# Delta operands stored by pairs of heads, last batches solved in a row, RWKV preparation with fewer products

## The chip, the cores and the metric

One Trainium2 chip, one core. The metric is the device time of one execution in microseconds: median 4167.8 of three runs. TensorE (PE), VectorE (DVE), ScalarE (ACT), GpSimd (POOL) and SyncE (SP, which here only issues DMAs) run their own instruction streams and meet at semaphores.

## The reference, cut to what matters

Two blocks in a row on x of 512 x 2048. The first (convolution, differential attention) and the second's input products are untouched. The change lies in the second block's mixers, each with 512 latent and 256 context tokens, in both directions, in chunks of 64:

```python
def gated_delta_chunked(q, k, v, beta, g, s0):        # 8 heads of 128
    decay = exp(where(tril, g_i - g_j, -inf))
    lmat = where(strict, (k * beta) @ k.T * decay, 0)
    tmat = inverse(eye + lmat)                        # a 64x64 system per head and chunk
    u, wk = tmat @ (v * beta), tmat @ (k * beta * exp(g))
    attn = where(tril, q @ k.T * decay, 0)
    def step(state, inp):                             # 12 chunks in order
        v_new = u_i - wk_i @ state
        o_i = q_i @ state + attn_i @ v_new
        state = state * exp(gl_i) + k_i.T @ v_new

def rwkv7_scan(r, w, k, v, kk, b_vec, s0):            # 16 heads of 64
    def step(state, inp):
        sa = -state @ kk_t
        state = state * w_t + sa x b_t + v_t x k_t
        return state, state @ r_t
# w_log = -softplus(-(w0 + tanh(wd) @ w_up)) - 0.5 ; decay = exp(-exp(w_log))
# so log(decay) = -exp(-0.5) * sigmoid(w0 + tanh(wd) @ w_up)
# context tokens only feed the state: in the last layer their outputs are not needed
```

The kernel brings the RWKV recurrence to chunks too: per chunk two 64x64 matrices from b and two from k (one of each against kk, one against r), and one system to invert.

## The kernel before

It runs in stages with a barrier between them: first block, second block's input products (`second`), `delta_prep`, `rwkv_prep`, `scans`, `closing`. P is 128 partitions, C = 64 tokens, NCH = 12 chunks (8 latent and 4 context), GH = 8 Delta heads, RP = 8 pairs of RWKV heads. A `Link` makes each DVE or POOL instruction wait for the one before it.

**delta_prep** (`DeltaPrep`) goes through the 8 heads; in a round, head i is finished while head i+1 is begun. It writes the head's operands into `ob[:, u]`, 12 x 579 floats a partition: for each direction 129 (`G_CH`: keys, queries, the chunk's decay), then 321 (`G_TOK`: masked matrix, values, tailed keys, beta). SP's `store` sends them to `g_scr` (chunk, head, partition, column) in pieces of 2316 bytes, and the systems' rows from `nb` in pieces of 256 bytes. `finish` waits for all stores before the barrier.

**rwkv_prep** (`RwkvPrep`) goes through 8 units of two heads, again with the next unit's beginning woven in. SP first issues `load_all` (six loads) and then each unit's seven (`load`, four of them gate weights). The DVE order is written out: `unit_keys`, `operands` for both directions, `mask` mb, `add_up` of the next unit, `mask` mk, `add_up`, `mask` mb, `add_bonus`, `mask` mk. The PE products that a `mask` reads wait for the mask before (`m_out`, one buffer `ps_m`). Meanwhile POOL solves systems, 96 at a time on 96 partitions (`solve`: load, wait, `invert`, store, wait): Delta's batch for both directions, then, once units 0 to 3 are stored, RWKV's first batch for both. The stage ends when POOL's last store has landed.

**scans** solves RWKV's second batch on POOL while the scans begin: `solve` d = 0, then d = 1, each waiting for its own load and store, in the one room `r.ops[0:96, 1]`. The loop takes steps n = 0 to NCH + LAG - 1 with LAG = 8: Delta's step n for n < 12 and RWKV's step n - 8 from n = 8. Steps 0 to 3 of each scan are context and produce no output. PE's order in a step: Delta keys, RWKV keys, `middle` and later `offdiagonal` of the next step's inverses, values, then `advance` by halves. RWKV's `middle` of step 0 therefore stands in step n = 7, before Delta's values. From n = 12 one tile of Delta's outputs a step is folded (`fold`, `take`, `add`). SP loads three inverses, then operands of two Delta steps, then in the loop operands of step n + 2 (two buffers, released by `free`); a step's operands are 2 x 528 KB in pieces of 516 bytes (`gchan`) and 2 x 657 KB in pieces of 1284 bytes (`gtok`). At n = LAG - 2 it waits for both solves (`y_out`) and loads RWKV's inverses and its step 1.

Of the kernel before, what the change touches and what calls it, by code (L numbers as in the profile page):

```python
# [21 lines left out]
P = 128  # L22
# [2262 lines left out]
class DeltaPrep:  # L2285
# [5 lines left out]
    def __init__(self, nc, st, k, p2, norms, gates_scr, g_scr, systems):  # L2291
        self.nc, self.k, self.p2, self.norms, self.gates_scr, self.g_scr, self.systems = nc, k, p2, norms, gates_scr, g_scr, systems
# [12 lines left out]
        self.ob = st.sb("ob", [P, 2, NCH, G_COLS])  # L2305
# [5 lines left out]
        self.x_in, self.stored = st.sems("x_in", 3), st.sems("stored", 2)  # L2311
# [135 lines left out]
    def heads(self, dve, i):  # L2447

        u = i % 2
        if i >= 2:  # L2450

            dve.wait_ge(self.stored[u], 48 * (i // 2))
        dve.wait_ge(self.s["eg_out"], 2 * i + 2)
        for d in range(2):
            self.tt(self.ob[:, u, :, G_CH * d:G_CH * d + 2 * C].rearrange("p c (j t) -> p c j t", t=C), self.kq[:, u],
                    self.eg[:, u, d].unsqueeze(2).to_broadcast([P, NCH, 2, C]))

    def weights(self, dve, i):
        u, em = i % 2, self.em[:, i % 2]
        beta = self.gb[:, 1, i, :]  # L2460
        self.link(self.nc.vector.tensor_scalar(self.ob[:, u, :, G_COLS - 1:G_COLS], self.over(beta, 1), 1.0, None, ALU.mult))
# [5 lines left out]
        self.tt(self.ob[:, u, :, 2 * G_CH:2 * G_CH + C], prod[:, :, 1, :], em)  # L2467
# [5 lines left out]
    def tails(self, dve, i):  # L2473
        u = i % 2
        dve.wait_ge(self.s["tok_k"], i + 1)
        self.tt(self.ob[:, u, :, 2 * G_CH + C + GD:2 * G_CH + C + 2 * GD], self.ps_t[:].rearrange("p (c v) -> p c v", v=GD),
# [11 lines left out]
    def exponentials(self, act_e, i):  # L2488
        u = i % 2
        act_e.wait_ge(self.s["em_ok"], i + 1)  # L2490
        if i >= 2:

            act_e.wait_ge(self.stored[u], 48 * (i // 2))
        self.alink(self.nc.scalar.activation(self.em[:, u], self.em[:, u], ACT.Exp))
        self.alink(self.nc.scalar.activation(self.tail[:, u], self.tail[:, u], ACT.Exp))
        self.alink(self.nc.scalar.activation(self.ob[:, u, :, G_CH - 1:2 * G_CH:G_CH], self.total[:, u], ACT.Exp))
        act_e.sem_inc(self.s["em_out"], 1)

    def values_out(self, act_e, i):
        act_e.wait_ge(self.s["tok_v"], i + 1)  # L2500
        self.alink(self.nc.scalar.activation(self.ob[:, i % 2, :, 2 * G_CH + C:2 * G_CH + C + GD],
# [3 lines left out]
    def store(self, sp, i):  # L2505
        u = i % 2
        sp.wait_ge(self.s["k_out"], i + 1)
        sp.dma_start(self.g_scr[:, i:i + 1].rearrange("c h p x -> p (c h) x"), self.ob[:, u]).then_inc(self.stored[u], 16)
        for d in range(2):
            rows = self.systems[d, 0:NCH * GH, :].rearrange("(c h) (s t) -> h s c t", h=GH, t=C)  # L2510
            sp.dma_start(rows[i:i + 1].rearrange("h s c t -> (h s) c t"),
                         self.nb[64 * d:64 * d + 64, u]).then_inc(self.stored[u], 16)

    def finish(self, sp):
        for u in range(2):
            sp.wait_ge(self.stored[u], 48 * GH // 2)


def delta_prep(nc, k, p2, norms, gates_scr, g_scr, systems):


    with Stage(nc, "gprep") as st:
        m = DeltaPrep(nc, st, k, p2, norms, gates_scr, g_scr, systems)
# [122 lines left out]

class RwkvPrep:
# [1197 lines left out]
```

## Time and profile before

| | us |
|---|---|
| median of three runs (lowest to highest) | 4167.8 (4160.57 to 4168.13) |
| the profiled execution, its own time | 4166.44 |
| its span, first to last instruction | 4164.7 |
| PE busy | 3582.6 (86%) |
| DVE busy | 2122.5 (51%) |
| ACT busy | 676.5 (16%) |
| POOL busy | 788.5 (19%) |
| mean granted TensorE clock | 0.917 of full speed |

Busy shares are means over stages with different limits: PE is the bound in the first block, and in the three stages changed here it is not. So they are read by stage.

### The profile page before, as it was taken

The page shows a single profiled execution, that of the slowest core. Times are in us where ns is not written, and L with a number is a line of the kernel's source. Part 1 is how long each engine was busy: PE and PEld are TensorE (multiplying, and loading weights), DVE is VectorE, ACT ScalarE, POOL GpSimd, SP SyncE. Part 2 cuts the span into 40 slices and gives each one's busy share as a digit, 9 for nine tenths or more (in the row PEclk, how much of TensorE's full clock was granted, in tenths as well). Part 3 has the DMA queues.
Part 4 walks back from the last instruction along what each step waited for, and adds up shares of the span by engine and source line. Part 5 has one row for each costly group of instructions (what it writes and reads, how often), then busy time and mean ns, then how long its engine had stood idle before and what let it go on. Part 6 is the DMA issues. An engine that isn't in the chain of part 4 may idle for free. (4 is left out here: it accounts for less than half of the span.)

```text
span 4164.7 us, 63954 instructions
## 1 busy us (share of the span) xinstructions
PE 3582.6 (86%) x28192; PEld 2855.1 (69%) x28192; DVE 2122.5 (51%) x2296; ACT 676.5 (16%) x1103; POOL 788.5 (19%) x819
## 2 busy tenths in 40 slices
PE   6999999999998988899999999865567545788888
PEld 3777777777887877788888888653455434677476
DVE  2577777733335455454633533354778643321464
ACT  2122222212000011201100000111223101211100
POOL 0111111110000000150052250001665766000000
PEclk8999999999999999999999999876788867888899
DMA  9444444444334353222322233256356798754242
GB/s 384 154 142 161 143 153 150 152 179 145 111 106 147 139 210 109 90 89 85 112 85 91 101 107 125 84 199 207 114 174 186 216 212 174 185 186 157 82 167 106
DMA packets 290469, 616.56 MB, mean 148 GB/s; under 512 B 117496, under 2 KB 184176, under 8 KB 258448
## 3 DMA queue, kind: packets, MB, share of 16 engines
q1 hardware_dynamic: 186736, 427.49, 31.1%
q0 software_dynamic: 21936, 95.56, 7.0%
q10 hardware_dynamic: 81520, 89.42, 6.4%
q8 instruction: 222, 3.64, 0.4%
q14 instruction: 55, 0.45, 0.0%
HBM read 472.02 MB, written 140.39 MB: 147 GB/s over the span
## 5 line engine op out<-in xcount | busy, mean ns | idle before, releaser
L180 PE MATMUL front_ps<-b_hT,p_wb 128*128 128x512 f32 x4224 | 980.6, 392 | 6.8 <-PEq L94 6.8
L180 PEld LDWEIGHTS front_ps<-b_hT,p_wb 128*128 128x128 f32 x4224 | 791.1, 188 | 187.3 <-issue 20.6
L1770 PE MATMUL in_ps<-b_hT,in_wb 128*128 128x512 f32 (+1 forms) x3264 | 750.1, 391 | 13.4 <-DVE in_wb L1757 13.4
L1770 PEld LDWEIGHTS in_ps<-b_hT,in_wb 128*128 128x128 f32 (+1 forms) x3264 | 607.1, 187 | 147.6 <-DVE in_wb L1757 13.6
L1755 DVE CAST in_wb<-in_raw 128x2048 fp32r<-128x2048 f32 (+1 forms) x68 | 82.6, 1215 | 535.9 <-PE in_ps L1770 530.9
L168 DVE CAST p_wb<-p_raw 128x2048 fp32r<-128x2048 f32 x88 | 108.0, 1227 | 431.7 <-PE front_ps L180 421.0
L811 POOL DMA_DIRECT2D front_mwb<-in_w_ada x128 | 101.0, 793 | 796.0 <-PE front_mps L821 791.2
L1770 PEld LDWEIGHTS in_ps<-b_hc,in_wb 128*128 128x128 f32 (+1 forms) x1728 | 211.4, 190 | 3.2
L1770 PE MATMUL in_ps<-b_hc,in_wb 128*128 128x256 f32 (+1 forms) x1728 | 212.6, 283 | 0.0
L170 DVE TENSOR_TENSOR p_wb<-p_raw,p_wb 128x2048 fp32r<-128x2048 f32 x88 | 201.7, 2293 | 3.0
L1209 PE MATMUL mid_ps<-mid_wb,b_hT 128*128 128x512 f32 x768 | 179.6, 395 | 13.7 <-DVE mid_wb L1194 13.7
L1079 PE MATMUL merge_ps<-b_hT,merge_wb 128*128 128x512 f32 x768 | 177.5, 394 | 12.3 <-DVE merge_wb L1067 10.1
L478 DVE SCALAR_TENSOR_TENSOR bf_both<-front_up,front_taps,bf_both 128x512 f32<-128x512 f32 x240 | 180.4, 752 | 11.8
L1209 PE MATMUL last_ps<-last_wb,last_pair 128*128 128x512 f32 x768 | 176.2, 392 | 11.5 <-DVE last_wb L1194 11.5
L1079 PEld LDWEIGHTS merge_ps<-b_hT,merge_wb 128*128 128x128 f32 x768 | 145.6, 190 | 44.2 <-DVE merge_wb L1067 10.5
L1209 PEld LDWEIGHTS mid_ps<-mid_wb,b_hT 128*128 128x128 f32 x768 | 145.6, 191 | 44.2 <-issue 14.1
L1209 PEld LDWEIGHTS last_ps<-last_wb,last_pair 128*128 128x128 f32 x768 | 145.5, 190 | 43.3 <-issue 13.0
L1757 DVE TENSOR_TENSOR in_wb<-in_raw,in_wb 128x2048 fp32r<-128x2048 f32 (+1 forms) x68 | 173.9, 2557 | 2.3
L2005 POOL TENSOR_TENSOR in_mdx<-in_mx 128x255 f32<-128x255 f32 (+9 forms) x53 | 59.0, 1114 | 526.2 <-ACT in_mx L1982 524.0
L2610 POOL TENSOR_TENSOR rprep_sn<-rprep_sn 96x62 f32<-96x62 f32 (+15 forms) x124 | 142.7, 1151 | 9.7
L2608 POOL TENSOR_TENSOR rprep_sn<-rprep_sn 96x62 f32<-96x62 f32 (+15 forms) x124 | 130.8, 1055 | 9.7
L1788 POOL MEMSET in_gper_row<- 128x2 f32 x1 | 0.1, 99 | 678.7 <-POOLq L94 678.7
(446 smaller groups left out, 4792.5 us busy)
## 6 DMA issues: line engine op xcount, KB each, us to landing
p_raw<-in_w_in_tiles SPq DMA_DIRECT2D x88, 1024.0 KB, 6.3
in_raw<-in_w_in_tiles SPq DMA_DIRECT2D x67, 1024.0 KB, 4.8
front_mwb<-in_w_ada POOLq DMA_DIRECT2D x128, 512.0 KB, 5.0
r_scr<-rprep_ob ACTq DMA_DIRECT2D x16, 2694.0 KB, 13.1
scan_rops<-r_scr SPq DMA_DIRECT2D x24, 1796.0 KB, 11.2
open_wb<-in_w_ada_groups SPq DMA_DIRECT2D x32, 1024.0 KB, 11.3
g_scr<-gprep_ob SPq DMA_DIRECT2D x8, 3474.0 KB, 11.0
merge_raw<-in_w_branch_units SPq DMA_DIRECT2D x32, 512.0 KB, 4.5
```

Of the source, the lines that this page charges most:

```text
L168: nc.vector.tensor_copy(self.wb[:, n % 2, 0], self.raw[:, n % 2]).then_inc(self.high_ok, 1)
L170: nc.vector.tensor_tensor(self.wb[:, n % 2, 1], self.raw[:, n % 2], self.wb[:, n % 2, 0].bitcast(F32), ALU.subtract).then_inc(self.w_split, 1)
L180: last = self.nc.tensor.matmul(self.ps[:, n % 2, :], self.wb[:, n % 2, x, kt, :], self.hT[:, y, kt, :], start=kt == term == 0, stop=kt == ...
L478: link(nc.vector.scalar_tensor_tensor(acc, u[:, j:j + T], self.taps[:, i, j:j + 1], acc, ALU.mult, ALU.add))
L811: pool.dma_start(self.wb[:, m % 2], w[m % 4, :, :, c:c + self.COLS]).then_inc(self.w_in[m % 2], 16)
L1079: last = self.nc.tensor.matmul(self.ps[:, u, :], self.wb[:, u, x, kt, :], self.pair[:, y, j, kt, :], start=kt == n == 0, stop=kt == self.C ...
L1209: last = self.nc.tensor.matmul(self.bank(i), self.pair[:, x, q * self.KQ + kt, t * P:(t + 1) * P], self.wb[:, n % 2, y, kt, :], start=q == ...
L1755: nc.vector.tensor_copy(high, raw).then_inc(self.high_ok, 1)
L1757: nc.vector.tensor_tensor(low, raw, high.bitcast(F32), ALU.subtract).then_inc(self.w_split, 1)
L1770: last = self.nc.tensor.matmul(self.ps[0:width, n % 3, first:end], self.wb[:, n % 2, x, kt, 0:width], h[:, y, kt, :], start=kt == term == ...
L2608: link(ops.tensor_tensor(t, y[:, :, a, j:j + 1].to_broadcast([BATCH, 2, na, ni]), y[:, :, j:j + 1, after].to_broadcast([BATCH, 2, na, ni]) ...
L2610: link(ops.tensor_tensor(y[:, :, a, after], y[:, :, a, after], t, ALU.subtract))
```

## The change

- Delta operands go to two tensors: `g_chan` (chunk, direction, partition, head, 129) and `g_tok` (chunk, partition, head, 321). `ob` holds two pairs of heads, with a pair's columns side by side. Heads 0 to 5 are stored by pairs after the odd head (pieces of 1032 and 2568 bytes), heads 6 and 7 singly (516 and 1284). Writers wait in `room`. A step's load in `scans` then reads 4128 and 10272 bytes in a piece. The exponential of the totals is issued once per direction.
- `rwkv_prep`: the factor -exp(-0.5) moves from a DVE multiplication into the scale of ACT's exponentials; the products and masks of context chunks are made only for the half that is used, the rest zeroed once at the start; gate weights of a unit come in one load from a re-laid input; `load_all` is issued by ACT.
- `scans`: LAG = 10; both solver loads are issued at once into two rooms (`r.ops[0:96, 0]` and `[0:96, 1]`), the inversions follow each other without waiting for a store; SP waits for the first store at n = 5 before RWKV's operands of step 0, and for the second at n = 9 before the inverses, ahead of Delta's last operands; the first loads are interleaved; the eight folds are spread by `tiles_at` over n = 12 to 20 (none at 16).

```diff
@@ DeltaPrep
+    def part(self, i, col, width):
+        at = col // G_CH * 2 * G_CH + i % 2 * G_CH + col % G_CH if col < 2 * G_CH else col + 2 * G_CH + i % 2 * G_TOK
+        return self.ob[:, i // 2 % 2, :, at:at + width]
+    def room(self, eng, i):
+        if i >= 2:
+            eng.wait_ge(self.n_stored[i % 2], 32 * (i // 2))
+        if i >= 4:
+            eng.wait_ge(self.stored[i // 2 % 2], 48 * (i // 4))
@@ store
-        sp.dma_start(self.g_scr[:, i:i + 1].rearrange("c h p x -> p (c h) x"), self.ob[:, u]).then_inc(self.stored[u], 16)
+        pair, done, hs = self.ob[:, i // 2 % 2], self.stored[i // 2 % 2], slice(i - 1, i + 1)
+        if i >= GH - 2:
+            for d in range(2):
+                sp.dma_start(self.g_chan[:, d, :, i, :].rearrange("c p x -> p c x"), self.part(i, G_CH * d, G_CH)).then_inc(done, 16)
+            sp.dma_start(self.g_tok[:, :, i, :].rearrange("c p x -> p c x"), self.part(i, 2 * G_CH, G_TOK)).then_inc(done, 16)
+        elif i % 2 == 1:
+            for d in range(2):
+                sp.dma_start(self.g_chan[:, d, :, hs, :].rearrange("c p h x -> p c (h x)"),
+                             pair[:, :, 2 * G_CH * d:2 * G_CH * (d + 1)]).then_inc(done, 16)
+            sp.dma_start(self.g_tok[:, :, hs, :].rearrange("c p h x -> p c (h x)"), pair[:, :, 4 * G_CH:2 * G_COLS]).then_inc(done, 16)
@@ RwkvPrep
-        for d in range(2):
-            for j, w in enumerate(self.ups):
-                sp.dma_start(self.up[:, u, j, d, :], w[d][:, rows(0)]).then_inc(self.x_in[u], 16)
+        sp.dma_start(self.up[:, u], self.ups[i]).then_inc(self.x_in[u], 16)
-        self.link(self.nc.vector.tensor_scalar(swd, swd, -math.exp(-0.5), None, ALU.mult))
-        self.alink(self.nc.scalar.activation(gx, gx, ACT.Exp))
+        self.alink(self.nc.scalar.activation(gx, gx, ACT.Exp, scale=-RATE))
@@ mask
-        self.tt(self.ob(i, d)[:, :, col:col + P], self.ps_m[:].rearrange("p (c x) -> p c x", x=P), mask)
+        for first, end, width in ((0, T // C, P), (T // C, NCH, C)):
+            self.tt(self.ob(i, d)[:, first:end, col:col + width], chunks[:, first:end, 0:width],
+                    mask[:, :, 0:width].to_broadcast([P, end - first, width]))
@@ matrix
-                      lambda r, c: self.ob(i, d)[r, c, self.AR:self.AR + P], self.ps_m, P)
+                      lambda r, c: self.ob(i, d)[r, c, self.AR:self.AR + (P if c < T // C else C)], self.ps_m, P)
@@ DeltaScan.load
-            sp.dma_start(self.chan[:, u, d], rows[:, :, G_CH * d:G_CH * (d + 1)]).then_inc(self.loaded[u], 16)
-            sp.dma_start(self.tok[r, u], rows[r, :, 2 * G_CH:G_COLS]).then_inc(self.loaded[u], 16)
+            sp.dma_start(self.chan[:, u, d], self.g_chan[STEPS[k][d], d]).then_inc(self.loaded[u], 16)
+            sp.dma_start(self.tok[r, u], self.g_tok[STEPS[k][d], r]).then_inc(self.loaded[u], 16)
@@ scans
-LAG = 8
+LAG = 10
+        tiles_at = lambda n: [t for t in range(GH) if NCH + t * LAG // GH == n]
-                for n in range(3):
-                    g.load_inverse(sp, n)
                 for n in range(2):
+                    g.load_inverse(sp, n)
                     g.load(sp, n)
-                r.load(sp, 0)
+                g.load_inverse(sp, 2)
                 for n in range(NCH + LAG):
+                    if n in (LAG - 5, LAG - 1):
+                        d = n // (LAG - 1)
+                        sp.wait_ge(solvers[d].y_out, 16)
+                        if d == 1:
+                            r.load_inverse(sp, 0)
+                        r.load(sp, d)
+                        if d == 1:
+                            r.load_inverse(sp, 1)
+                            r.load_inverse(sp, 2)
-                    if n == LAG - 2:
-                        sp.wait_ge(solver.y_out, 32)
-                        for m in range(3):
-                            r.load_inverse(sp, m)
-                        r.load(sp, 1)
@@ POOL in scans
-                for d in range(2):
-                    solve(nc, pool, link, solver, systems, 2, d, d)
+                for d, m in enumerate(solvers):
+                    pool.dma_start(m.rows, rows[d]).then_inc(m.n_in, 16)
+                for d, m in enumerate(solvers):
+                    pool.wait_ge(m.n_in, 16)
+                    invert(pool, nc.gpsimd, Link(pool, m.chain), m, d)
+                    pool.sem_inc(m.tick, 1)
+                    pool.dma_start(rows[d], m.rows).then_inc(m.y_out, 16)
```

## Rows read from the trace of the kernel before

**Rows 1.** Windows: us, then busy time per engine (instructions), clock, DMA share, GB/s.

```profile
2663.00:2888.30 225.30, 146.25 (x1312) 106.28 (x1312) 127.29 (x151) 36.32 (x49) 0.00 (x0) 0.73 0.52 181
2888.30:3347.00 458.70, 267.62 (x3632) 213.23 (x3632) 327.67 (x269) 123.90 (x137) 295.55 (x272) 0.78 0.57 175
3347.00:3964.00 617.00, 440.78 (x9552) 358.02 (x9552) 211.71 (x296) 104.37 (x215) 138.56 (x184) 0.80 0.63 166
```

**Rows 2.** Timeline of PE, Delta alone: start, us, engine, line, operation, [idle before <- releaser].

```profile
3372.23 3.68 PE L3117 MATMUL scan_gwork<-scan_gstate,scan_gchan 128*64 128x128 f32 x32 [11.21 <-issue]
...
3385.66 1.97 PE L3117 MATMUL scan_gwork<-scan_gstate,scan_gchan 128*64 128x128 f32 x16
...
3460.55 3.68 PE L3117 MATMUL scan_gwork<-scan_gstate,scan_gchan 128*64 128x128 f32 x32 [5.52 <-DMA scan_gtok<-g_scr]
...
3476.16 1.09 PE L3117 MATMUL scan_gwork<-scan_gstate,scan_gchan 128*64 128x128 f32 x16
...
3529.05 1.07 PE L3292 MATMUL scan_ro<-scan_rinv 32*32 32x32 f32 x64 [30.58 <-DMA scan_rinv<-systems]
```

**Rows 3.** Waits, 3347 to 3546: who waited for what, us in total, times, longest.

```profile
PE scan_gwork L3117 <- DMA scan_gtok<-g_scr: 23.5, 5, 8.2
```

**Rows 4.** DMA by queue, windows 3362:3372, 2876:2882, 2884:2887: packets, MB, share of 16 engines.

```profile
q1 hardware_dynamic: 2856, 2.12, 114.7%
...
q1 hardware_dynamic: 1002, 2.32, 101.9%
...
q1 hardware_dynamic: 1683, 0.62, 88.1%
```

**Rows 5.** Timeline of SP and POOL in the scan stage.

```profile
3347.09 9.88 SPq L3081 DMA_DIRECT2D scan_ginv<-systems  x6
...
3523.87 8.68 SPq L3277 DMA_DIRECT2D scan_rinv<-systems  x12
...
3357.37 0.21 POOL L2601 MEMSET scan_rops<- 96x64 f32 x1 [9.32 <-DMA scan_rops<-systems]
...
3436.64 0.54 POOL L2626 DMA_DIRECT2D scan_rops<-systems  x1 [11.66 <-DMA systems<-scan_rops]
...
3450.28 0.21 POOL L2601 MEMSET scan_rops<- 96x64 f32 x1 [13.10 <-DMA scan_rops<-systems]
...
3516.52 0.53 POOL L2630 DMA_DIRECT2D systems<-scan_rops  x1 [0.57 <-POOL scan_rops L2620]
```

**Rows 6.** Timeline of DVE: beginnings of steps 8 and 10, ends of 11 and 19.

```profile
3545.38 0.69 DVE L3210 TENSOR_TENSOR scan_gy<-scan_gtok,scan_gwork 128x512 f32<-128x512 f32 x1 [0.32 <-DVE scan_gstate L3231]
...
3617.62 1.52 DVE L3210 TENSOR_TENSOR scan_gy<-scan_gtok,scan_gwork 128x512 f32<-128x512 f32 x2 [0.32 <-DVE scan_rstate L3404]
...
3684.03 0.69 DVE L3404 TENSOR_TENSOR scan_rstate<-scan_rstate,scan_rops 128x512 f32<-128x512 f32 x1
...
3900.17 0.69 DVE L3404 TENSOR_TENSOR scan_rstate<-scan_rstate,scan_rops 128x512 f32<-128x512 f32 x1
```

**Rows 7.** Windows of tile scan_ro alone, one step of RWKV alone; columns as above.

```profile
3740.00:3768.00 28.00, 8.75 (x320) 8.38 (x320) 1.37 (x2) 1.88 (x5) 0.88 0.54 172
```

**Rows 8.** Timeline of POOL, PE and DVE in rwkv_prep.

```profile
3158.53 0.53 POOL L2626 DMA_DIRECT2D rprep_sn<-systems  x1 [68.87 <-DMA r_scr<-rprep_ob]
...
3070.77 5.36 PE L2838 MATMUL rprep_ps_m<-rprep_ob,rprep_kT 64*64 64x128 f32 x48 [5.80 <-issue]
...
3078.63 0.82 DVE L2766 TENSOR_SCALAR rprep_sw<-rprep_sw 128x768 f32<-128x768 f32 x1 [0.71 <-ACTq L2751]
...
3090.18 1.76 DVE L2731 TENSOR_TENSOR rprep_ob<-rprep_ps_m,all_mask 128x1536 f32<-128x1536 f32 x1 [3.86 <-PE rprep_ps_m L2838]
...
2906.25 1.01 DVE L2742 SCALAR_TENSOR_TENSOR rprep_kk<-rprep_k_in,rprep_vec,rprep_ps_n 128x768 f32<-128x768 f32 x1 [15.36 <-DMA rprep_up<-in_rwkv_a_up]
```

**Rows 9.** Timeline of SP at delta_prep's end, and the next stage's first load.

```profile
2874.46 0.36 SPq L2508 DMA_DIRECT2D g_scr<-gprep_ob  x1
...
2888.29 0.33 SPq L2695 DMA_DIRECT2D rprep_inv<-norms  x1
```

More of the change, by code:

```diff
@@ L2460, in weights @@
         beta = self.gb[:, 1, i, :]
-        self.link(self.nc.vector.tensor_scalar(self.ob[:, u, :, G_COLS - 1:G_COLS], self.over(beta, 1), 1.0, None, ALU.mult))
+        self.link(self.nc.vector.tensor_scalar(self.part(i, G_COLS - 1, 1), self.over(beta, 1), 1.0, None, ALU.mult))
         dve.wait_ge(self.s["em_out"], i + 1)
@@ L2490, in exponentials @@
         act_e.wait_ge(self.s["em_ok"], i + 1)
-        if i >= 2:
-            act_e.wait_ge(self.stored[u], 48 * (i // 2))
+        self.room(act_e, i)
         self.alink(self.nc.scalar.activation(self.em[:, u], self.em[:, u], ACT.Exp))
         self.alink(self.nc.scalar.activation(self.tail[:, u], self.tail[:, u], ACT.Exp))
-        self.alink(self.nc.scalar.activation(self.ob[:, u, :, G_CH - 1:2 * G_CH:G_CH], self.total[:, u], ACT.Exp))
+        for d in range(2):
+            self.alink(self.nc.scalar.activation(self.part(i, G_CH * d + G_CH - 1, 1), self.total[:, u, :, d:d + 1], ACT.Exp))
         act_e.sem_inc(self.s["em_out"], 1)
@@ L2837, in products @@
                 r = slice(64 * h, 64 * h + 64)
-                last = self.nc.tensor.matmul(ps[r, c * width:(c + 1) * width], lhs[r, c * C:(c + 1) * C], rhs(r, c), start=True, stop=True)
+                x = rhs(r, c)
+                last = self.nc.tensor.matmul(ps[r, c * width:c * width + x.shape[-1]], lhs[r, c * C:(c + 1) * C], x, start=True, stop=True)
         last.then_inc(self.s[sem], 1)
@@ L2990, in _ @@
             def _(act_e):
+                m.load_all(act_e)
                 m.start_act(act_e)
@@ L3596, in r_output, with scans @@
         link(nc.vector.tensor_tensor(o, o, self.zr[:, t], ALU.mult))
-LAG = 8
-def scans(nc, k, p2, gain, vectors, bonus, g_scr, r_scr, v_scr, systems, slots, late, yT):
+LAG = 10
+def scans(nc, k, p2, gain, vectors, bonus, g_chan, g_tok, r_scr, v_scr, systems, slots, late, yT):
     with Stage(nc, "scan") as st:
-        g = DeltaScan(nc, st, g_scr, systems, slots)
+        g = DeltaScan(nc, st, g_chan, g_tok, systems, slots)
         r = RwkvScan(nc, st, r_scr, v_scr, systems, yT[:, GH:2 * GH])
         out = HeadOutputs(nc, st, k, p2, gain, vectors, bonus, g, r, late, yT)
-        solver = Solver(st, "sp", r.ops[0:BATCH, 1].rearrange("p d q x -> p (d q x)"))
+        solvers = [Solver(st, f"sp{d}", r.ops[0:BATCH, d].rearrange("p d q x -> p (d q x)")) for d in range(2)]
+        tiles_at = lambda n: [t for t in range(GH) if NCH + t * LAG // GH == n]
         in_g = lambda n: 0 <= n < NCH
@@ L3700, in _ @@
                         g.store(act_e, n)
-                    if n >= NCH:
-                        out.take(act_e, n - NCH)
+                    for t in tiles_at(n):
+                        out.take(act_e, t)
                 out.root(act_e)
@@ L3740, in _ @@
             def _(pool):
-                link = Link(pool, solver.chain)
-                for d in range(2):
-                    solve(nc, pool, link, solver, systems, 2, d, d)
+                rows = [systems[d, 2 * BATCH:3 * BATCH, :] for d in range(2)]
+                for d, m in enumerate(solvers):
[5 more added lines that the diff above has]
+                    pool.dma_start(rows[d], m.rows).then_inc(m.y_out, 16)
                 for n in range(NCH):
```

80 lines of the change are left out of this document (43 added, 37 removed).

## The prediction

> **What bounds the kernel now.** Read first the busy time by stage [rows 1], since the change touches three of five stages. In none of the three is an engine full: PE is busy for 146 of 225 us in delta_prep, 268 of 459 in rwkv_prep, 441 of 617 in scans. So each is bound by a chain of waits, and the next views are timelines and waits.
>
> In scans the reader is to see three things. The stage's first load is issued at 3347.09, but Delta's first keys start only at 3372.23, 25.1 us later [rows 2, 5]. In the Delta-alone part PE waits 23.5 us in five places for `gtok` [rows 3]. And at 3529.05 it has stood 30.58 us for RWKV's inverses [rows 2], which SP may load only when POOL's second store has landed, at 3523.87 [rows 5]. All three lie on the path: Delta's and RWKV's steps are serial, and nothing else runs there. The DMA view says why `gtok` is late: with pieces of 516 and 1284 bytes the queue moves 2.12 MB in 10 us while full, 56 ns a piece on 16 engines; with pieces of 2316 bytes it moves 2.32 MB in 6 us, 96 ns a piece or 387 GB/s [rows 4]. A Delta step has 3072 such pieces, 10.8 us of a full queue, in a step of 13.4 us (3372.23 to 3385.66) that must also carry inverses and POOL's 1.57 MB loads and stores.
>
> rwkv_prep ends with POOL: its third inversion waits 68.87 us for the stores of units 0 to 3 and begins its load at 3158.53 [rows 8]; from there two solves take 188.6 us to the next stage's beginning at 3347.09 [rows 5]. What DVE does after unit 3 has slack. delta_prep ends when its last stores have landed: issued at 2874.46, next stage at 2888.29 [rows 9].
>
> **delta_prep: +6.** Heads 0 to 5: the same bytes in 1.5 times as many pieces, hidden by a round of 25 us; the writers' waits for `nb` are met a round later at most. ACT's added instruction stands in idle time. DVE's count stays. Heads 6 and 7 are on the path: a single store has 3 x 1536 pieces instead of 1536. If bytes alone count, it takes as now, 1536 x 96 / 16 = 9.2 us: +0. If each piece costs the 56 ns of the scan's loads, 4608 x 56 / 16 = 16.1 us; the seventh then is still running when the eighth is issued at 2874.5 (about 15.5 us after it), and the end moves by 7 + 2.5 = 9 to 10. Pieces of 256 bytes were written at 25 ns (1683 in 3 us, 88.1%) [rows 4], so 516 bytes should lie between: I take +6, keep 0 and +10.
>
> **rwkv_prep: -13.** What counts is when unit 3 is stored. Three terms. (a) The start: the first keys wait until 2906.25 for gate weights, the last of seven loads behind six others in SP's queue [rows 8], 18 us after the stage's first load [rows 9]. Two issuers instead of one, and ten issues before this point instead of thirteen; but the same bytes pass, POOL's 1.57 MB beside them. I take -3, between 0 and -7. (b) The DVE multiplication, 0.82 us in the row [rows 8], two a unit, five units before this point. The one before mask mk only lengthens DVE's wait for PE's products (5.36 us) and is worth 0; the other, after ScalarE's 0.71 us wait, shortens the chain: -0.9 a unit. (c) The products: 16 of 48 instructions halve in width, a sixth of 5.36 = 0.9 us [rows 8]. The stage's mean granted clock is 0.78 [rows 1]; if 5.36 is a product at 1.2 GHz, one at 2.4 saves 0.45, so 0.7 on average. DVE waits for two of four products a unit (3.86 us before the last mask) [rows 8]: -1.4 a unit. The masks become two instructions for 1280 instead of 1536 columns, worth 0. Sum: (0.9 + 1.4) x 4 + 0.9 + 3 = 13, range -3 to -20 (every product and multiplication on the path). POOL's two solves behind it keep their 188.6. If DVE's work, 31 us earlier at its end, were late instead, the gain would be the same or less; it is cut too.
>
> **scans: -52.** I lay the new time line from the stage's first load, T.
> - Delta's first keys. Ahead of them: inverses 0 (0.26 MB), operands 0 (2.37 MB), and now both of POOL's loads (3.1 MB). At 387 GB/s [rows 4] that is 15 us, plus 4 for issue, latency and the half inverses: T+19 instead of T+25.1. From T+11 (POOL's loads behind) to T+25.
> - Steps 0 to 9 alone. A step without output is 13.4 us, one with output 15.6 (3460.55 to 3476.16) [rows 2]: 4 x 13.4 + 6 x 15.6 = 147. `gtok`'s 23.5 us go, since a step's pieces shrink to 2.37 MB / 387 = 6.1 us, plus 2 to 3 of latency, within 13.4. RWKV's operands of step 0 (4.1 MB, 10.6 us) stand in SP's queue from n = 5; Delta's of step 7 are wanted a step later, and fit. Keep +12 for half the waits left.
> - RWKV's middle and offdiagonal in step 9: the middle is 1.07 us [rows 2], I take 3.
> - The solver. Load 10.3 (3347.09 to 3357.37), inversion 67.1 (to 3424.4, which is 3436.64 less its waits), inversion 66.2 (3450.28 to 3516.52), store 7.4 (to 3523.87) [rows 5]: T+151. The waits of 11.66 and 13.10 between are what the change removes. DVE stands still less than before and POOL should suffer for it: +5, T+156. Inverses need 5.2 more (3523.87 to 3529.05) [rows 2, 5]: T+162. PE wants them after step 9's keys, T+19+53.6+78+4 = T+155: a stall of 7 instead of 30.6. Queued behind the waiting SP at n = 9 are Delta's operands of step 11; they are wanted over 30 us later.
> - Two steps with both: steps 8 and 9 took 72.2, 10 and 11 67.1 (to 3684.72) [rows 6]. I take 70.
> - RWKV alone. Eight output steps, 216.2 from 3684.72 to 3900.86 [rows 6], stay: 216. Two more without output: the mean is 27.0, less output's part of 8.75 us that PE spends on `scan_ro` in 320 instructions, 192 of them output [rows 7]: between 5.3 and 8.75, I take 7. So 20 each, 40.
> Sum 19 + 147 + 3 + 7 + 70 + 216 + 40 = 502 against 553.8 now (3347.09 to 3900.86). So LAG = 10 alone costs: two alone-steps (31) and two without Delta (40) for two joint ones (70) is +1, and it buys cover for the solver. The tail of 63 us is untouched.
>
> **Sum.** 6 - 13 - 52 = -59 on the profiled execution's 4166.4 (its span is 4164.7): **4107 us**. That execution is 1.4 us under the median 4167.8, within their spread.
>
> The Trainium skill speaks against this change in "DMA: Bandwidth & Descriptors", section "Specifications": line rate is reached from 512 bytes a transfer on. Both old kinds of piece are above that. The rows of the scan's loads differ: full queue, about 213 GB/s at a mean of 742 bytes, 387 at 2316 [rows 4]. By the rule merging gives nothing and the single stores cost nothing: rival 1 below, about 4130. I go by the rows.
>
> **The rivals.**
> 1. *The Delta loads are not late through their pieces* but through issue and latency (SP's issues of `ginv` alone take 9.88 us for six [rows 5]). Then the 23.5 and the 6 of the start stay and the stores' +6 goes: 4107 + 30 - 6 = 4131. Against it: the queue is full in the waiting windows [rows 4]. 5%.
> 2. *The solver stays the gate.* POOL in rwkv_prep needs more: two solves in 188.6, less load, store and waits of some 25 to 30, is 80 an inversion. At 80 here, the stall is 2 x 13.5 - 5 = 22 longer: 4129. For it: DVE's busier steps; against: both inversions here took 66 to 67 [rows 5]. 12%.
> 3. *More comes than I count*: stores +0, rwkv_prep -20, start T+12, joint steps 67: 4107 - 6 - 7 - 7 - 3 = 4084. 15%.
> 4. *Slower than before*: the same solver, past its point. Each us of it after T+150 is a us of the end, for PE stands in step 9 with Delta and RWKV behind it. Free of stall, the path has 59 + 7 = 66 us in hand; beyond T+151+66 = T+217 the kernel is slower than before: inversions of 100 us. At 104 it is about 4175. Nothing in the rows shows above 80. 3%.
> 5. *It does not do what it says*: a layout or queue effect that keeps the gains of scans near zero, with a delta_prep that costs 10: 4160 to 4170. 4%.
>
> **How the numbers follow.** Forecast 61%, and rivals 5, 12, 15, 3, 4%. Its own range is 4093 to 4121 from the kept ends. For 8 in 10 I reach to rivals 3, 1 and 2 in part: 4084 to 4135. From no change a measurement of this kernel tells about 0.2%, 8.3 us: faster 0.94, same 0.03, slower 0.03.
>
> **What would show it.** Right: no wait for `gtok` before step 10; first Delta keys near 19 us after the stage's first load; POOL's inversions back to back, SP released near T+156, PE's wait for RWKV's inverses under 10 us; the third solve's wait about 13 us shorter; delta_prep 6 us longer. Wrong: waits for `gtok` under a queue that isn't full (1), inversions near 80 (2), RWKV steps without output longer than 25, or a third solve that starts no earlier, which would mean that neither products nor multiplication paced unit 3.

## The result

| | before | after |
|---|---|---|
| median, us (runs) | 4166.44 (4) | 4138.76 (4: 4137.45 to 4147.18) |
| profiled execution, us | 4166.44 | 4139.95 |
| span, us | 4164.7 | 4138.2 |
| mean granted clock | 0.917 | 0.921 |

Ratio of after to before 0.9941, 95% interval 0.9927 to 0.9956: 27.7 us faster in the medians. I forecast 4107, 59 faster, in a range of 4084 to 4135: the sign was right, the size half of it, and the time 4 us outside the range.

The same windows by stage as [rows 1], of the changed kernel (columns as there):

```profile
2661.00:2896.40 235.40, 145.22 (x1312) 106.05 (x1312) 127.29 (x151) 37.95 (x57) 0.00 (x0) 0.73 0.64 173
2896.40:3348.50 452.10, 250.74 (x3632) 200.06 (x3632) 303.41 (x291) 123.97 (x137) 292.24 (x272) 0.77 0.59 177
3348.50:3937.60 589.10, 436.20 (x9552) 353.42 (x9552) 214.14 (x296) 104.49 (x215) 139.97 (x184) 0.83 0.62 174
```

delta_prep is 10.1 longer, rwkv_prep 6.6 shorter, scans 27.9 shorter. PE's waits in scans from Delta's first keys to step 10, against [rows 3] and the last row of [rows 2] (columns: who waited for what, us in total, times, longest); the last two rows are the kernel before, 3347 to 3560:

```profile
PE scan_ro L3316 <- DMA scan_rinv<-systems: 15.2, 1, 15.2
PE scan_gwork L3185 <- DVEq L3256: 12.0, 5, 3.8
PE scan_gwork L3141 <- DMA scan_gtok<-g_tok: 10.6, 5, 5.8
PE scan_gwork L3141 <- DVEq L3256: 6.9, 6, 2.0
...
PE scan_gwork L3161 <- DVEq L3232: 9.6, 4, 3.0
...
PE scan_gwork L3117 <- DVEq L3232: 3.3, 3, 2.1
```

The waits for the operands halved (23.5 to 10.6), the stall for RWKV's inverses halved (30.6 to 15.2), and PE's waits for DVE grew by 6.0 (12.9 to 18.9). The timeline of SP, POOL and PE tells that the stall isn't the solver's:

```profile
3494.18 0.54 POOL L3776 DMA_DIRECT2D systems<-scan_rops  x1 [0.58 <-POOL scan_rops L2640]
...
3521.12 0.33 SPq L3096 DMA_DIRECT2D scan_gchan<-g_chan  x1
...
3523.15 1.35 SPq L3105 DMA_DIRECT2D scan_ginv<-systems  x2
3524.54 9.36 SPq L3301 DMA_DIRECT2D scan_rinv<-systems  x4
...
3537.95 1.07 PE L3316 MATMUL scan_ro<-scan_rinv 32*32 32x32 f32 x64 [15.19 <-DMA scan_rinv<-systems]
```

POOL stores the last batch at T+145.7 (T is the stage's first load, 3348.53), three us ahead of my line; SP asks for the inverses 30 us later, right behind Delta's operands of step 10, which step 8 releases at 3521. The first keys came not at T+19 but T+26.9, and rwkv_prep's first multiplication of keys on DVE not earlier but later:

```profile
3375.44 3.68 PE L3141 MATMUL scan_gwork<-scan_gstate,scan_gchan 128*64 128x128 f32 x32 [6.29 <-issue]
...
2918.69 1.01 DVE L2764 SCALAR_TENSOR_TENSOR rprep_kk<-rprep_k_in,rprep_vec,rprep_ps_n 128x768 f32<-128x768 f32 x1 [17.27 <-PE rprep_ps_n L2854]
```

The second row is T+22.2 of its stage (from 2896.47); in [rows 8, 9] it was 2906.25, T+18.0.

### The profile page after: what moved, and what is told of

Same layout as the page of the kernel before. It is cut to its first block and busy times, and to the rows that moved or that the text cites. A ratio compares the mean times of both kernels' runs of the same rounds, so it can differ in the third digit from the quotient of the medians.

```text
span 4138.2 us, 63966 instructions
## 1 busy us (share of the span) xinstructions
PE 3560.4 (86%) x28192; PEld 2834.4 (68%) x28192; DVE 2101.3 (51%) x2318; ACT 678.6 (16%) x1111; POOL 787.4 (19%) x819
## 5 line engine op out<-in xcount | busy, mean ns | idle before, releaser
L1770 PEld LDWEIGHTS in_ps<-b_hT,in_wb 128*128 128x128 f32 (+1 forms) x3264 | 606.8, 187 | 147.2 <-DVE in_wb L1757 13.5
L1079 PE MATMUL merge_ps<-b_hT,merge_wb 128*128 128x512 f32 x768 | 178.8, 395 | 12.4 <-DVE merge_wb L1067 10.2
L1079 PEld LDWEIGHTS merge_ps<-b_hT,merge_wb 128*128 128x128 f32 x768 | 146.2, 191 | 44.9 <-DVE merge_wb L1067 10.6
L1209 PEld LDWEIGHTS last_ps<-last_wb,last_pair 128*128 128x128 f32 x768 | 145.4, 189 | 43.3 <-issue 12.9
## 6 DMA issues: line engine op xcount, KB each, us to landing
front_mwb<-in_w_ada POOLq DMA_DIRECT2D x128, 512.0 KB, 4.9
scan_rops<-r_scr SPq DMA_DIRECT2D x24, 1796.0 KB, 11.1
open_wb<-in_w_ada_groups SPq DMA_DIRECT2D x32, 1024.0 KB, 11.2
merge_raw<-in_w_branch_units SPq DMA_DIRECT2D x32, 512.0 KB, 4.6
mid_raw<-in_w_o_parts SPq DMA_DIRECT2D x32, 512.0 KB, 3.7
```

The lines of the kernel that those rows point to most:

```text
L1079: last = self.nc.tensor.matmul(self.ps[:, u, :], self.wb[:, u, x, kt, :], self.pair[:, y, j, kt, :], start=kt == n == 0, stop=kt == self.C ...
L1209: last = self.nc.tensor.matmul(self.bank(i), self.pair[:, x, q * self.KQ + kt, t * P:(t + 1) * P], self.wb[:, n % 2, y, kt, :], start=q == ...
L1770: last = self.nc.tensor.matmul(self.ps[0:width, n % 3, first:end], self.wb[:, n % 2, x, kt, 0:width], h[:, y, kt, :], start=kt == term == ...
```

## The experiments

All are edits of the changed kernel. The first line of each is the ratio to the kernel before with its interval. A kernel's time varies by 10 to 30 us between executions (the twelve of e8 lie between 4139 and 4169), as much as a part is worth; so the parts are read from the stages of the profiled executions, set side by side here. One execution can lie at the end of its series: the profiled one was the slowest in e1, e3, e7 and e12 and the fastest in e4 and e15. "Keys" is Delta's first keys and "loop" DVE's end of RWKV's last step, both from the scan stage's first load.

| | delta_prep | rwkv_prep | keys | loop |
|---|---|---|---|---|
| before | 225.2 | 458.8 | 25.1 | 553.8 |
| after | 235.4 | 452.1 | 26.9 | 527.3 |
| e1_inverse_first | 228.5 | 455.7 | 27.4 | 528.3 |
| e2_gates_on_sp | 229.7 | 446.1 | 28.3 | 526.6 |
| e3_full_products | 234.4 | 452.1 | 28.3 | 537.6 |
| e4_old_layout | 220.0 | 450.1 | 28.8 | 532.0 |
| e5_halves_together | 231.1 | 451.9 | 32.8 | 532.7 |
| e6_pool_loads_later | 229.5 | 452.4 | 23.3 | 534.7 |
| e7_rwkv_start | 229.9 | 434.6 | 27.5 | 531.2 |
| e8_multiplication_kept | 230.2 | 459.3 | 27.2 | 524.6 |
| e9_one_token_load | 229.4 | 453.5 | 23.7 | 505.8 |
| e10_no_inversions | 229.5 | 456.4 | 34.7 | 534.3 |
| e11_best_new_layout | 234.5 | 431.3 | 27.4 | 524.7 |
| e12_best_old_layout | 227.0 | 436.9 | 29.2 | 540.2 |
| e13_by_steps | 238.6 | 453.2 | 24.2 | 509.9 |
| e14_best_by_steps | 239.1 | 434.3 | 24.0 | 512.0 |
| e15_best_by_steps_pool | 234.9 | 432.1 | 19.9 | 512.1 |

The same code gives delta_prep 228.5 to 235.4, rwkv_prep 450.1 to 456.4, and the loop 524.6 to 537.6 (after, e2, e3, e7, e8: mean 529.5). A single difference under 7 us in the first two columns, or under 13 in the last, shows nothing by itself.

**e1_inverse_first**: 0.9926 (0.9911 to 0.9940).

```diff
-                    if n in (LAG - 5, LAG - 1):   # d = 1: wait, inverse 0, load 1, inverses 1, 2
+                    if n == LAG - 2:
+                        sp.wait_ge(solvers[1].y_out, 16)
+                        r.load_inverse(sp, 0)
+                    if n == LAG - 1:              # load 1, inverses 1, 2
```

> The changed kernel, with RWKV's first inverses asked for one iteration earlier in SP's program (n = 8, before Delta's operands of step 10) and the rest at n = 9 as now. Theory: the solver isn't late; its last store is issued at 3494.18, but SP issues the four loads of inverses only at 3524.54, because the loads of step 10 stand before them and are released by step 8. They should now be issued near 3510, the 15.2 us that PE waits for them in step 9 fall under 2, and the kernel take about 4138.8 - 14 = 4125, 0.990 of the kernel before. Rival (the solver is the gate, as I predicted): SP waits in the same place for the store, the wait stays above 12 us and the time stays within 3 us of 4139.

The stall went (0.8 us), and 14 us did not come: the loop took 528.3, the median is 6 us under the changed kernel's by the ratios, with overlapping intervals. Steps 9 and 10 of the changed kernel, then of e1 (windows, columns as in [rows 1]):

```profile
3520.90:3556.70 35.80, 17.84 (x352) 13.39 (x352) 8.86 (x15) 5.75 (x13) 1.22 (x4) 0.71 0.91 236
3556.70:3587.20 30.50, 25.36 (x654) 21.73 (x656) 10.16 (x16) 8.14 (x17) 1.22 (x4) 0.89 0.35 80
```
```profile
3523.30:3549.00 25.70, 18.66 (x352) 12.96 (x352) 8.83 (x15) 5.74 (x13) 1.21 (x4) 0.80 1.05 283
3549.00:3582.60 33.60, 26.84 (x654) 21.75 (x656) 10.20 (x17) 8.13 (x17) 1.21 (x4) 0.85 0.43 98
```

Step 9 gained 10.1 us, steps 10 and 11 gave back 3.8 (step 11 took 33.2 for 32.5), and 5.7 were lost before step 9, where the code is the same. So the stall's removal is worth some 6 us in this execution, and the loop's end hides it. In step 9 PE now stood 5.3 us in the middle of its products, with no wait, while 3.6 MB passed:

```profile
3530.18 0.43 PE L3172 MATMUL scan_go<-scan_gy,scan_gtok 64*64 64x128 f32 x2
3535.91 0.69 PE L3172 MATMUL scan_go<-scan_gy,scan_gtok 64*64 64x128 f32 x2 [5.30 <-issue]
```

So the solver isn't the gate (rival 2 falls), and the stall is worth less than its 15 us.

**e2_gates_on_sp**: 0.9942 (0.9924 to 0.9961). **e7_rwkv_start**: 0.9910 (0.9895 to 0.9925).

```diff
             @block.sync
+                m.load_all(sp)
                 for i in range(RP):
             @block.scalar
-                m.load_all(act_e)
             @block.gpsimd
+                pool.wait_ge(m.x_in[0], 64)       # e7 alone
```

> The changed kernel, with the six loads of norms, low rows and vectors back on SP ahead of the units' loads, where they were before; the gate weights stay one load. Theory: on their own queue these small loads shared the DMA engines with 3.5 MB of unit loads, so the last came at T+19 instead of T+14 (T: the stage's first load), and the first gate product began at T+23.4 instead of T+19.2. Back on SP it begins near T+17 and rwkv_prep takes 6 us less (446), the kernel 4133, 0.9925. Rival (the single gate load or the long memsets pace the start): the first product stays past T+21, and the time within 2 us of 4139.

> The changed kernel, with the small loads of rwkv_prep back on SP ahead of the units' and POOL's first load held until unit 0 has landed. Theory: as with gates_on_sp, the small loads land first; besides, POOL's 16 KB rows no longer stand beside unit 0. First gate product near T+13 instead of T+23.4 (gates_on_sp tells the first part), rwkv_prep 9 to 10 us shorter than 452, since POOL's third solve waits 60 us for the units and has room for a later start: 4129, 0.992. Rival (POOL's own chain becomes late: its wait of 63.2 us shrinks by its later start but the stores come no earlier): 452 stays.

The first keys' multiplication comes at T+18.0 and T+11.5 instead of T+22.2, the stage takes 446.1 and 434.6. The two rows of e7, that multiplication and POOL's third load:

```profile
2903.72 1.01 DVE L2764 SCALAR_TENSOR_TENSOR rprep_kk<-rprep_k_in,rprep_vec,rprep_ps_n 128x768 f32<-128x768 f32 x1 [6.53 <-DMA rprep_up<-in_rwkv_up_tiles]
...
3138.38 0.54 POOL L2646 DMA_DIRECT2D rprep_sn<-systems  x1 [33.35 <-DMA r_scr<-rprep_ob]
```

In e7 the third solve still waits 33.35 us for the units, so the later start of POOL costs nothing. The five runs with this start take 433.9 in the mean, the eight with the changed kernel's code 453.2: 19 us of the stage, more than the whole change brought there; by the ratios e7 is 13 us under the changed kernel. e2's kernel time doesn't show the 6 us that I expected (0.9942 for 0.9941, with 8 us of interval either way).

**e3_full_products**: 0.9965 (0.9953 to 0.9977). **e8_multiplication_kept**: 0.9974 (0.9961 to 0.9987).

```diff
-                      lambda r, c: self.ob(i, d)[r, c, self.AR:self.AR + (P if c < T // C else C)], self.ps_m, P)
+                      lambda r, c: self.ob(i, d)[r, c, self.AR:self.AR + P], self.ps_m, P)      # e3, with one mask
+        self.link(self.nc.vector.tensor_scalar(swd, swd, -math.exp(-0.5), None, ALU.mult))      # e8
```

> The changed kernel with the masked products at full width and one mask instruction each, as before. My prediction priced the narrower products at 1.4 us a unit, 5.6 up to the store of unit 3: POOL's third load in rwkv_prep should come at T+270.3 instead of T+264.7 and the kernel take 4144.5. Rival (products are hidden behind DVE; what shortened the units is the multiplication): T+265 and no difference, 4139.

> The changed kernel with DVE's multiplication of the decay by -exp(-0.5) kept, two a unit, as before. With the full products the third load came no later (T+264.7), so what made the units shorter by 9.8 us (5.5 plus the 4.3 by which the start is later) should be the multiplication: third load at T+272, rwkv_prep near 460, kernel 4146, 0.996. Prediction's price: 0.9 us a unit and 0.9, 4.5 in all: T+269, 4143.5. Rival (the stage varies by this much from execution to execution): T+265, 4139.

POOL's third load, in e3 from 2894.96 (T+264.7, as after) and in e8 from 2891.87 (T+270.8):

```profile
3159.62 0.54 POOL L2646 DMA_DIRECT2D rprep_sn<-systems  x1 [65.15 <-DMA r_scr<-rprep_ob]
```
```profile
3162.69 0.53 POOL L2646 DMA_DIRECT2D rprep_sn<-systems  x1 [65.63 <-DMA r_scr<-rprep_ob]
```

In the eight runs whose stage has the changed kernel's code this load comes at T+263.2 to T+268.5, mean T+265.7. So the multiplication is worth about 5 (one run, 2 over the highest of the eight), and the products nothing that shows, where I had priced them at 5.6. e3's whole time is longer in its scans, whose code is the same.

**e4_old_layout**: 0.9948 (0.9931 to 0.9964). DeltaPrep and the loads of DeltaScan as before the change.

> The changed kernel with Delta's operands kept as before, one tensor and one store a head, all else changed. Prediction's price of the layout: delta_prep -10 (measured now), scans +30 at most (23.5 of waits for operands and 6 of the start). Theory after the trace of the changed kernel: the new layout's loads move only about 250 GB/s, not 387, waits of 10.6 us remained and the start was not earlier, so it is worth 23.5 - 10.6 = 13 in scans; delta_prep falls from 235.4 to 225.3; net +3: 4142. Rival 1 of the prediction (pieces don't matter): the waits stay near 10, and the kernel takes 4129. Rival by the prediction's price: 4139 + 30 - 10 = 4159.

delta_prep 220.0 (the three with the old layout: mean 224.1; the eleven with pairs: 231.1), PE's waits for the operands 22.4 us, loop 532.0. The layout costs 7 in delta_prep and gives 2.5 in scans by this execution, which was the fastest of its six, 9 us under their median; e11 and e12 below differ by 15.5. By the ratios of the whole kernel, 0.9948 against 0.9941, it is worth 3 us net, within the intervals: nothing that can be told.

**e5_halves_together**: 0.9981 (0.9966 to 0.9996).

```diff
+    def load_far(self, act_e, k):            # on ACT, at the end of step k - 2
+        act_e.dma_start(self.tok[64:128, u], self.g_tok[STEPS[k][1], 64:128]).then_inc(self.loaded[u], 16)
```

> The changed kernel, with the load of Delta's token operands for direction 1 (partitions 64 to 127) on ACT's queue, so that it runs beside the one of direction 0 (partitions 0 to 63) instead of after it. Theory: in the changed kernel a 10272-byte row of these loads takes 0.776 us of a DMA engine (13.2 GB/s an engine), while RWKV's 14368-byte rows, which go to all 128 partitions, take 0.590 (24.4); what slows them is that a load fills one half of the partitions at a time. Together the 128 rows should take near 0.45 us each, the waits of PE for the operands fall from 10.6 to 14.6 us to under 4, and scans take about 10 us less: 4130, 0.992. Rival (16 DMA engines are simply full, 250 GB/s is what they do beside the solver's traffic): rows stay at 0.75 us, waits stay above 9, time 4139.

Slower than the changed kernel, and no test of the halves: on the two queues the halves overlapped for about 2 of 5 us, a row still took 0.75, and ACT's load at the start stood before Delta's first inverses (keys T+32.8).

**e9_one_token_load**: 0.9898 (0.9881 to 0.9915). **e13_by_steps**: 0.9939 (0.9925 to 0.9952).

```diff
-            sp.dma_start(self.tok[r, u], self.g_tok[STEPS[k][d], r]).then_inc(self.loaded[u], 16)
+            if d == 0:                           # e9; in e13 from self.g_tok[k], stored by step
+                sp.dma_start(self.tok[:, u], self.g_tok[STEPS[k][0]]).then_inc(self.loaded[u], 16)
```

> The changed kernel, with one load of Delta's token operands over all 128 partitions in place of two over 64 each; direction 1 so gets direction 0's chunk, the same bytes (this part of the output is wrong, its time isn't touched by values). halves_together didn't tell: the two halves overlapped only in part. Theory: in a load of 64 partitions a 10272-byte row takes 0.776 us because only half of the partitions take data; over 128 it takes near 0.42 (RWKV's rows: 24.4 GB/s an engine). A step's operands land in 7 us instead of 9.6, the waits of PE for them fall from 10.6 to under 4, and scans take 585. Rival: rows stay above 0.7 us, waits 10, scans 589.

> The changed kernel, with Delta's token operands kept by step instead of by chunk: a step's 128 rows (direction 0 in partitions 0 to 63, direction 1 in 64 to 127) stand together and are fetched by one load over all partitions; delta_prep stores them in four parts, each from 64 partitions. Theory: scans as in one_token_load, first keys at T+23.7 and T+506 at the loop's end instead of T+527; the stores of delta_prep are slower by half-partition reads, hidden but for heads 6 and 7, +4: 4139 - 21 + 4 = 4122, 0.9905. Rival (the stores from halves back up through the rounds): delta_prep +15 or more, no gain.

In e9 direction 1 gets the rows of direction 0's chunk: the same bytes with other contents. This settles what slowed the rows. The DMA queue while almost only these rows pass (packets, MB, share of 16 engines, which is the time the packets took): in the changed kernel 1.8 us from 3400.7, in e9 2.5 us from 3387.5, and beside them RWKV's operands in the changed kernel, 5 us from 3470, to all 128 partitions:

```profile
q1 hardware_dynamic: 34, 0.34, 92.5%
...
q1 hardware_dynamic: 304, 2.00, 96.9%
```
```profile
q1 hardware_dynamic: 103, 1.01, 97.1%
```

The queue is full in all three, at 188, 406 and 410 GB/s. The same 10272-byte row takes 0.776 us (mean over a step's load) into 64 partitions and 0.39 into 128. PE's waits for the token operands are gone, keys come at T+23.7, and the loop is 23.7 us under the mean of the same code; by the ratios the kernel is 18 us under the changed one, intervals apart:

```profile
PE scan_gwork L3186 <- DVEq L3257: 14.1, 5, 3.8
PE scan_ro L3317 <- DMA scan_rinv<-systems: 12.9, 1, 12.9
PE scan_gwork L3142 <- DVEq L3257: 8.0, 6, 2.4
PE scan_gwork L3142 <- issue: 3.1, 1, 3.1
PE scan_gwork L3142 <- DMA scan_gchan<-g_chan: 3.1, 3, 1.6
```

e13 fetches the right rows in the same way: 0.39 us a row, loop 509.9, 19.6 less, but its stores now leave from half the partitions, and delta_prep takes 238.6, 7.5 more. Net it should be 12 faster than after; the median is 10 less, the ratio to before is the same. That e13 is faster than the changed kernel isn't shown by times, only by stages.

**e6_pool_loads_later**: 0.9961 (0.9946 to 0.9977).

```diff
+                pool.wait_ge(g.inv_in[0], 32)
                 pool.dma_start(solvers[0].rows, rows[0])
-                pool.dma_start(solvers[1].rows, rows[1])
+                    if n == 1:                   # on SP
+                        sp.dma_start(solvers[1].rows, rows[1]).then_inc(solvers[1].n_in, 16)
```

> The changed kernel, with POOL's first load in scans held until Delta's first inverses have landed and the second issued by SP at n = 1 instead of at the start. Theory: POOL's two loads, 192 rows of 16 KB at 1.12 us, stand in every DMA engine beside SP's 256-byte pieces and hold Delta's first inverses until T+17.6 (T: the stage's first load) and the first keys until T+26.9; now the inverses land by T+5 and the keys begin near T+18, 9 us earlier. The solver begins some 4 us later and isn't awaited, as RWKV's inverses are asked for at n = 9 anyhow. Kernel 4130, 0.992. Rival (bytes alone count, the order is worth nothing; or what is gained comes back as a longer wait for RWKV's inverses): first keys past T+24, or scans within 3 us of 589 though the keys are early.

Keys at T+23.3, 3.6 earlier; Delta's first inverses had landed by T+3.5 instead of T+17.6. From there PE waited 16.8 us more for Delta's operands, later operands were late by 21.2 us in four steps, and the loop took 534.7: the rival.

**e10_no_inversions**: 0.9956 (0.9941 to 0.9971). The line `invert(...)` of scans left out.

> The changed kernel without the two inversions of POOL in scans; its loads and stores of the systems stay (RWKV's last chunks then use matrices that aren't inverted; the output is wrong). It prices what POOL's work costs the other engines. Theory: Delta's steps with output take 17 us while POOL inverts and 14.6 after (3506.3 to 3520.9), for DVE's products of state and decay take 1.4 to 1.5 us beside POOL and 0.71 alone; four such steps and a little in the others give 10 us: Delta's step 9 ends near T+397 - 389 = 198 instead of 208 after the stage's first load, scans 579, kernel 4129. Rival (the steps are long for their loads, not for POOL): less than 3 us. The waits for RWKV's inverses stay, as SP asks for them at n = 9 in any case.

DVE's product of state and decay, in the changed kernel and without POOL's work (busy us, mean ns | idle before):

```profile
L3252 DVE TENSOR_TENSOR scan_gstate<-scan_gstate,scan_gchan 128x512 f32<-128x512 f32 x48 | 46.7, 973 | 54.6 <-PE scan_go L3172 52.5
```
```profile
L3252 DVE TENSOR_TENSOR scan_gstate<-scan_gstate,scan_gchan 128x512 f32<-128x512 f32 x48 | 33.2, 692 | 56.7 <-PE scan_go L3172 54.7
```

DVE loses 13.5 us to POOL, and the first two steps with output fell from 17.7 and 17.1 us to 14.9 and 16.0. The kernel gained nothing: the next load was waited for 10.6 us, the first keys came at T+34.7, and from the first keys to the loop's end it took 499.6, against 500.4. My reading is that the loads set the pace and hide POOL's price; no run takes both away, so this isn't shown.

**e11_best_new_layout**: 0.9901 (0.9886 to 0.9916). **e12_best_old_layout**: 0.9911 (0.9897 to 0.9926). e7's start with

```diff
+                    if n == LAG - 2:             # inverses 0; inverses 1 at LAG - 1 behind step 11's operands
+                    if n == LAG:                 # operands 1, inverses 2
```

> The changed kernel with what the runs point to: rwkv_prep's small loads on SP ahead of the units', POOL's first load there after unit 0 (measured: 438 instead of 452), RWKV's first inverses in scans asked for at n = 8, and the others spread: inverses 1 at n = 9, operands 1 and inverses 2 at n = 10, so that 6.7 MB aren't queued at once in step 9, where PE stood 5.3 us without a wait in the middle of its products. Expected: -14 from rwkv_prep, and of the 15.2 in scans at least 10: 4139 - 14 - 10 = 4115, 0.9885. Rival (the spread loads are late for step 11, or the Delta steps take the gain back as in inverse_first): 4125, as rwkv_start alone.

> The same as best_new_layout, with Delta's operands kept as before the change. Measured in old_layout: delta_prep 9 to 10 us shorter (222.6 against 232 in the mean of the profiled executions), scans 2 to 5 longer. Expected: 4110, some 5 us under best_new_layout. Rival (freed of the wait for the inverses, Delta's steps go by their loads, 22.4 us of waits in the old layout against 10.6): equal or slower than best_new_layout.

e11 has e7's gain alone; the wait for the inverses moved to step 10 (11.2 us). With the old layout (e12) the loop is 540.2, 15.5 longer, and delta_prep 7.5 shorter; the ratios' intervals overlap, so the two layouts can't be told apart.

**e14_best_by_steps**: 0.9898 (0.9884 to 0.9912). **e15_best_by_steps_pool**: 0.9891 (0.9878 to 0.9905).

e14 is e13 with e7's start and RWKV's first inverses asked for at n = 8, the others spread over n = 9 and 10; e15 adds e6's order of POOL's loads.

> by_steps with rwkv_start's order of loads (-14) and RWKV's inverses 0 asked for at n = 8, inverses 1 at the head of n = 9, operands 1 and inverses 2 at n = 10. With Delta's loads at 7 us a step there is room for them; the 12.9 us that PE still waited for RWKV's inverses in one_token_load should go, and step 10 stay at 31. Expected: 4122 - 14 - 11 = 4097, 0.9845. Rival (PE's wait only moves to the next step, as in best_new_layout): 4108.

> best_by_steps with POOL's first load in scans after Delta's first inverses and the second issued by SP at n = 1, as in pool_loads_later. There the first keys came 3.5 us earlier and the gain was lost to loads that were late. With short loads: first keys near T+19, 4 us earlier, kept: 4093. Rival (the second load now collides in steps 1 to 3, or the solver, 10 us later, becomes the gate at n = 8): equal to or slower than best_by_steps.

Both beat before and after: by the ratios e15 stands 45 us under before and 21 under after (0.9891 against 0.9941, intervals apart). Both miss what I expected: e14 0.9898 for 0.9845, and e15 equals e14, its rival. In e15 the keys came at T+19.9, but a wait of 11.1 us for RWKV's inverses was back and the loop was as long. In e14 no wait for RWKV's inverses is left, and the loop is as long as e13's, with its 12.4. The windows show where the gain went (steps 9, 10, 11 of e13, then of e14):

```profile
3519.70:3550.60 30.90, 17.32 (x354) 13.31 (x354) 8.82 (x14) 5.74 (x13) 1.21 (x4) 0.72 0.95 274
3550.60:3576.40 25.80, 23.54 (x656) 19.77 (x656) 10.20 (x16) 8.13 (x17) 1.21 (x4) 1.00 0.26 95
3576.40:3609.00 32.60, 27.90 (x617) 22.67 (x615) 11.04 (x16) 6.63 (x13) 1.21 (x4) 0.84 0.45 148
```
```profile
3502.30:3523.60 21.30, 17.78 (x352) 12.52 (x352) 8.82 (x14) 5.74 (x13) 1.22 (x4) 0.84 0.56 155
3523.60:3556.90 33.30, 28.39 (x656) 23.19 (x656) 10.20 (x16) 8.13 (x17) 1.21 (x4) 0.80 0.62 216
3556.90:3590.20 33.30, 27.72 (x616) 22.41 (x614) 11.03 (x16) 6.63 (x13) 1.21 (x4) 0.85 0.44 145
```

Behind a stall step 10 runs at 1.00, all of it at 2.4 GHz, with the DMA engines busy for 0.26, and takes 25.8; without the stall it gets 0.80, with the DMA engines busy for 0.62, and takes 33.3, with 4.9 us more of PE's products and 2.9 and 2.0 of stops in PE's issue. Clock and stops changed together, and no run parts them; in the changed kernel step 10 also stood behind a stall, and got 0.89 and 30.5. Of the 9.6 us that step 9 lost, 8.2 come back in steps 10 and 11.

## Why the prediction was half right

By its own terms, in the profiled execution: 33 us of the forecast 59 are missing, 4 in delta_prep, 6 in rwkv_prep and 26 in scans, less 3 that came outside these terms.

- **delta_prep, +6**: 10 in that execution, 7.0 in the mean of eleven. Right, within the kept ends of 0 and 10. The stores of the last two heads kept the engines full from 2857.3 to 2893.7, 12105 packets at 54 ns, near the 56 of my dearest case, and the reading "bytes alone" fell. My 25 ns for a 256-byte piece came from a window that held pieces of 2316 bytes as well; alone the median is 18.
- **rwkv_prep, -13**: -6.7. The start, taken at -3, was +4.2 (e2 and e7: the small loads, on a queue of their own, shared the engines with the units' loads and POOL's 16 KB rows). I counted issues and not what stands in the DMA engines beside them; the range, 0 to -7, had no loss in it. The multiplication, taken at -4.5, measured about -5. The products, taken at -5.6, are 0: DVE's waits for them were 22.0 us in the changed kernel and 21.2 with full products (e3), so a shorter product bought nothing. POOL's third solve waited 63.2 us for 68.9, 5.7 less and not 13. The parts sum to about -1; the rest of the -6.7 is as large as what the stage varies by, and stays open.
- **scans, -52**: -26.5 at the loop's end. First keys T+26.9 for T+19: 8 missing. Steps 0 to 9, from first keys to 3557.0, 181.6 for 157: 25 missing, of which waits for operands 10.6 (I had 0) and the stall 15.2 (I had 7); the other 6 have the size of what PE's waits for DVE grew by, which I left out (18.9 us here, 12.6 without POOL's inversions in e10). Joint steps 64.3 for 70; RWKV alone 254.6 for 256. LAG = 10 itself was sized rightly.

**The step that failed** is one sentence of the scans: "a step's pieces shrink to 2.37 MB / 387 = 6.1 us". The 387 GB/s of [rows 4] was a store from all 128 partitions. Over half of the bytes of Delta's loads, the token operands, goes to 64 partitions at a time, and there a larger piece helps little: in the medians of the trace's packets up to step 10, 1284 bytes took 0.111 us in the kernel before (11.6 GB/s an engine), 10272 bytes 0.791 after (13.0). The rest, to all 128, gained from size: 516 bytes took 0.039 us and 4128 take 0.187 (13.2 and 22). So the mean of 213 GB/s had two causes, and I took one for both. e9 takes away the other alone, and the loop falls to 505.8, against the 502 of my sum and the 529.5 of the same code; it comes near 502 with a stall of 12.9 that I had at 7 and shorter joint steps, so in part by luck. That the layout brought 2.5 us in e4, and 15.5 between e11 and e12, and not 29, is the same error. The 387 GB/s sized the start too: POOL's two loads, to 96 partitions, took 1.12 us for a 16 KB row, so 13.4 us for 3.1 MB instead of 8.

The Trainium skill has the rule I didn't look for: "SBUF — State Buffer", section "Door 1: The DMA port swizzle (why `[64,N]` ≈ `[32,N]`)", says that bandwidth goes by how many of 16 ports the partitions reach, and that partitions 0 to 63, or 64 to 127, reach eight. The traces agree: 188 GB/s against 410. The rule I did weigh, "DMA: Bandwidth & Descriptors", section "Specifications", line rate from 512 bytes on, does not hold here: 516-byte pieces moved at 0.6 of the rate of 4128-byte ones in these medians.

Rival 1 had its 5% for another reason and ended nearest, at 4131: the loads stayed late, but the queue was full. Rival 2, the solver as gate, was wrong (POOL was done at T+146); I had the right wait and the wrong cause, for I compared only when POOL ends and not where SP stands in its own program: I wrote that step 11's operands queue behind the inverses and missed that the inverses queue behind step 10's. Two inversions in a row took 135 us, the 67 each that I had. Worth of that cause: 6 us in e1 and 1 in e14, since the steps behind gave the rest back. Of rival 3's assumptions three were false, and the fourth came, with joint steps of 64.3 under its 67; 4 and 5 did not come.

Open: which part of the change gave the 26.5 us that scans did gain (no run has the solves in a row without LAG = 10, or LAG = 10 without them), what part of a step's length behind a removed stall is clock and what part stops, and why PE stops inside a loop of products for 2 to 5 us while the queue is full.

## What to carry to other kernels

A rate read from a transfer to 128 partitions didn't hold for one to 64 (410 GB/s against 188), so read a full queue's rate for each shape by itself before sizing a merge. A small load put on a queue of its own wasn't ahead of the large ones (4.2 us later here than in front of them on one queue). And a stall taken away can come back in the next steps, here 8.2 of 9.6 us, so read their granted clock and DMA share before counting it in full. Before calling a part's worth, look where the profiled execution lies among its series.

## What was not expected of the hardware

- A 16 KB row of POOL's loads into 96 partitions held an engine for 1.12 us (14.6 GB/s an engine), and Delta's first inverses, 256-byte pieces beside 192 such rows, were there 17.6 us after the stage's first load, without them after 3.5.
- Step 10 of the scans took 25.8 us at a granted clock of 1.00 (e13) and 33.3 at 0.80 with stops in PE's issue (e14), with the same instructions.
- DVE's product of 128 x 512 with a broadcast operand took 692 ns in the mean without POOL's inversions and 973 with them, over the same 48 products.
- The same stages of the same code varied by 6 to 13 us from execution to execution while their neighbours stayed.
